# The down pieces of a mixture of experts on a second DMA queue, with rows that lie side by side

## What is computed

```python
def expert_block(args):
    e, tok, wt = args
    xb = h_pad[tok]
    gu = xb @ w_gu[e] + b_gu[e]                      # w_gu: 32 x 1024 x 2048
    gate = jnp.minimum(gu[:, :D_FF], SWIGLU_LIMIT)
    up = jnp.clip(gu[:, D_FF:], -SWIGLU_LIMIT, SWIGLU_LIMIT)
    act = (up + 1.0) * gate * jax.nn.sigmoid(SWIGLU_ALPHA * gate)
    y = act @ w_down[e] + b_down[e]                  # w_down: 32 x 1024 x 1024
    return y * wt[:, None].astype(y.dtype)
```

## Time and profile before

| | |
|---|---|
| median of 3 runs | 1272.31 us (1272.03 to 1273.51) |
| the profiled execution | 1272.04 us, its span 1270.2 us |
| PE busy | 1167.3 us, 92% of the span |
| DVE, ACT, POOL busy | 431.1, 126.8, 93.5 us |
| bytes moved by DMA | 459.96 MB, 362 GB/s over the span |
| queue q1 (SP's) | 458.50 MB |
| queue q10 (ACT's) | 1.08 MB |
| granted clock of PE | 0.984 of full speed on average |

### The profile page before, as it was taken

One profiled execution on the slowest core, in us unless ns is written; L12 is line 12 of the kernel. 1 busy time (PEld: TensorE's weight loads), 2 busy tenths in 40 slices (PEclk: granted clock), 3 DMA queues, 4 the chain that ended last, 5 costly groups with the idle time before them and its releaser, 6 DMA issues.

```text
span 1270.2 us, 17813 instructions
## 1 busy us (share of the span) xinstructions
PE 1167.3 (92%) x6940; PEld 491.0 (39%) x6940; DVE 431.1 (34%) x824; ACT 126.8 (10%) x254; POOL 93.5 (7%) x116
## 2 busy tenths in 40 slices
PE   5999898995999999999999999999999999999997
PEld 1765676853333333333333333333333333333332
DVE  3785784125222233222222222222233222222224
ACT  3101112213100000000000000000000000000001
POOL 1503653002000000000000000000000000000000
PEclk8999899996999999999999999999999999999999
DMA  9999314563899999999999999999999999999991
GB/s 356 367 411 387 108 67 151 190 228 145 324 416 417 418 418 418 418 418 418 418 418 418 417 418 418 418 417 417 417 417 417 417 417 419 418 418 418 414 417 58
DMA packets 95588, 459.96 MB, mean 362 GB/s; under 512 B 13565, under 2 KB 13801, under 8 KB 59721
## 3 DMA queue, kind: packets, MB, share of 16 engines
q1 hardware_dynamic: 93992, 458.50, 89.4%
q10 hardware_dynamic: 1568, 1.08, 0.3%
HBM read 458.51 MB, written 1.05 MB: 362 GB/s over the span
## 4 chain that ended last, share of the span: by engine, by line
PE 45%; DMA 22%; SPq 18%; DVE 2%; issue 2%; ACT 1%; DVEq 0%
DMA ring<-in_w_down 22%; PE ps L762 17%; SPq L334 13%; PE ps L803 8%; SPq L329 5%; PE ps L464 4%; PE ps L745 3%; PE ps L619 2%; PE ps L657 2%; PE ps L687 2%; PE ps L754 1%; PE ps L591 1%; PE ps L784 1%; PE ps L494 1%; PE ps L791 0%
## 5 line engine op out<-in xcount | busy, mean ns | idle before, releaser
L803 PE MATMUL ps<-ring,tmp 128*64 128x512 f32 x1024 | 241.3, 601 | 48.5 <-DMA ring<-in_w_down 38.6
L762 PE MATMUL ps<-ring,zone 128*64 128x512 f32 x1024 | 232.2, 595 | 0.0
L762 PE MATMUL ps<-zone 128*64 128x512 f32 x896 | 207.5, 596 | 0.3 <-DVE zone L1294 0.3
L1340 DVE TENSOR_TENSOR x_tok<-x_tok,ps 128x512 f32<-128x512 f32 x128 | 82.0, 682 | 261.9 <-PE ps L745 261.9
L803 PEld LDWEIGHTS ps<-ring,tmp 128*64 128x64 f32 x1024 | 67.6, 136 | 201.7 <-issue 126.8
L762 PEld LDWEIGHTS ps<-ring,zone 128*64 128x64 f32 x1024 | 70.7, 137 | 151.5 <-issue 151.4
L762 PEld LDWEIGHTS ps<-zone 128*64 128x64 f32 x896 | 61.5, 137 | 136.1 <-issue 134.8
L464 PE MATMUL ps<-hT,ring 128*128 128x256 f32 x448 | 103.1, 390 | 2.7 <-ACT hT L856 2.7
L1334 DVE TENSOR_TENSOR tmp<-ps,zone 128x512 f32<-128x512 f32 x32 | 22.1, 692 | 226.7 <-PE ps L803 226.7
L935 ACT ACTIVATE hT<-hT 128x512 f32<-128x512 f32 x32 | 20.2, 630 | 785.4 <-DVE hT L1353 785.4
L464 PEld LDWEIGHTS ps<-hT,ring 128*128 128x128 f32 x448 | 86.2, 195 | 20.2 <-issue 8.4
(11 more groups left out here) (270 smaller groups left out, 830.1 us busy)
## 6 DMA issues: line engine op xcount, KB each, us to landing
ring<-in_w_gu SPq DMA_DIRECT2D x128, 1024.0 KB, 21.6
ring<-in_w_down SPq DMA_DIRECT2D x128, 1024.0 KB, 24.2
zone<-in_w_gu SPq DMA_DIRECT2D x112, 1024.0 KB, 19.6
ring<-in_w_ada SPq DMA_DIRECT2D x24, 1024.0 KB, 16.5
ring<-in_w_in SPq DMA_DIRECT2D x16, 1024.0 KB, 14.8
xs<-in_w_gu SPq DMA_DIRECT2D x16, 1024.0 KB, 20.4
ring<-in_w_glu SPq DMA_DIRECT2D x4, 1024.0 KB, 11.5
ring<-in_w_out SPq DMA_DIRECT2D x4, 1024.0 KB, 4.8
```

What stands on the lines that cost most here:

```text
L762: last = mm(ps[CAP * h:CAP * h + CAP, b, :], hg[:, j, :], w[:, 0, D * b + 512 * h:D * b + 512 * h + 512], start=False, stop=(j == GU_PIECE ...
L803: last = mm(ps[CAP * h:CAP * h + CAP, 3, :], actT[:, k % 4, k // 4, :], wk[:, 512 * h:512 * h + 512], start=False, stop=(j == DN_PIECES - ...
L1340: V.tensor_tensor(x_tok[:, t, 512 * h:512 * h + 512], x_tok[:, t, 512 * h:512 * h + 512], ps[:, 6 + h, :], ALU.add).then_inc(S["comb_add"], 1)
```

## The change

The down pieces are issued by ACT, which has a DMA queue of its own. ACT does it at the head of each item, ahead of the sigmoid, with the same wait for `w_used`. SP issues only gate/up pieces from item 2 on, in the order of items; the down pieces of item 0 stay with SP. The rows of w_down are spread otherwise: with a row number written as 512h + 4p + q, partition p gets for each piece the two rows q and q + 1 that lie side by side, 8 KB in one run. For the products to fit, transpose j takes every fourth column of `act_`, starting with j. The bytes, the slots and PE's instructions are the same in number and order.

```diff
+    def down_rows(e, j):
+        k = DN_ROWS[j]
+        return w_down[0, bass.ds(e, 1)].rearrange("e (h p q) n -> p (e h) q n", h=2, p=P)[:, k // 4, k % 4:k % 4 + 2, :]
...
             def load_dn(e, j):
-                k = DN_ROWS[j]
-                src = w_down[0, bass.ds(e, 1)].rearrange("e (k p) n -> p (e k) n", p=P)[:, k:k + 2, :]
-                sp.dma_start(dn_slot(j), src).then_inc(dn_in[j], 16)
+                sp.dma_start(dn_slot(j), down_rows(e, j)).then_inc(dn_in[j], 16)
...
-            def next_dn(i, e):
-                for j in range(DN_PIECES):
-                    sp.wait_ge(w_used, i * PASS + (PRE - PASS + GU_PIECES + j + 1))
-                    load_dn(e, j)
-
-            with sp.Fori(1, EXPERTS // 2 - 1) as q:
+            with sp.Fori(1, EXPERTS // 2) as q:
                 next_gu(2 * q, 2 * q, 0)
-                next_dn(2 * q - 1, 2 * q - 1)
                 next_gu(2 * q + 1, 2 * q + 1, 1)
-                next_dn(2 * q, 2 * q)
-            e = EXPERTS - 2
-            next_gu(e, e, 0)
-            next_dn(e - 1, e - 1)
-            next_dn(e, e)
-            next_gu(e + 1, e + 1, 1)
-            next_dn(e + 1, e + 1)
...
-                    last = nc.tensor.transpose(ps[:, j // 2, P * (j % 2):P * (j % 2) + P], act_[:, P * j:P * j + P], ident)
+                    last = nc.tensor.transpose(ps[:, j // 2, P * (j % 2):P * (j % 2) + P], act_[:, :].rearrange("p (n q) -> p q n", q=4)[:, j, :], ident)
...
+            def load_dn(i, e):
+                for j in range(DN_PIECES):
+                    act.wait_ge(w_used, i * PASS + (PRE - PASS + GU_PIECES + j + 1))
+                    act.dma_start(dn_slot(j), down_rows(e, j)).then_inc(dn_in[j], 16)
...
             with act.Fori(1, EXPERTS) as i:
+                load_dn(i, i)
                 item(i)
```

More of the change, by code:

```diff
@@ L385, in _ @@
                             next_gu(2 * q + par, e, par)
-                            next_dn(2 * q + par, e)
             for i in range(TT):
@@ L952, in _ @@
                     with act.If(i < count):
+                        load_dn(i, act.value_load(itab[0:1, bass.ds(i, 1)], min_val=0, max_val=EXPERTS - 1))
                         item(i)
```

## The result

The changed kernel takes 1260.06 us, median of four runs (1258.76 to 1261.54), against 1272.49 us for the kernel before in the same session. The ratio is 0.9902, with a 95% interval of 0.9884 to 0.9919. The prediction was 1260. Its profiled execution took 1260.16 us, with a span of 1258.3 us, 11.9 less than before.

A forecast was written before the change was run, and what follows sets the result against it. The prediction took the DMA stream's bytes and rate to bound the kernel from 350 to 1240 us. 1272.04 less 8.6 for rate and 3.5 for the tail gave 1259.9, said as 1260 us, range 1249 to 1269.

The forecast's parts named there:

- The bound: From 350 to 1240 us bytes and rate set the time; only rate, holes and PE's work after the last byte count.
- The rate term: 8 KB runs for w_down save 0.072 us a piece over 120 pieces from 350 us on: 8.6 us.
- The second queue: PE's four waits for w_down go; each pass's last gate/up piece comes 2.1 us late; the middle moves no time.
- The tail: From the last byte to the end of the down products: 15.0 us instead of 18.5, saving 3.5 us.
- The sum: Whole kernel: 1272.04 - 8.6 - 3.5 = 1259.9, stated as 1260 us; chance 0.58 for 1255 to 1265.
- The transposes: L791's weight loads 16 bytes apart cost 0 to 1.7 us a pass, covered by PE's 2.1 us wait; taken as 0.
- a sign of being wrong: The forecast is wrong if a pass in which PE has no waits lasts longer than 27.7 us.
- Rows alone: Rival: only the faster rate from w_down's new rows holds, the split does nothing; 1263.4 us, chance 0.11.
- tail alone: Rival: only the shorter tail holds, w_down being slow for another reason than its runs; 1268.5 us, chance 0.06.
- The rule on issuing engines: Trainium skill: starting DMAs from several engines saves only sequencer time; by it the split gives nothing, leaving 1263.4 us.

The follow-up runs named there:

- columns side by side: The changed kernel with the transposes of before, taking 128 columns side by side, so its output is another one: 1260.27 us, ratio 0.991.

## Why the prediction was right, step by step

- **The bound.** Right. Rate, holes and tail account for every kernel of the table: 890 us are bytes, and PE's waits in the middle move from one line to another without moving the end.
- **The rate term.** Right in cause, shown twice: new rows alone give 422 GB/s on one queue, and 4 KB runs on the other matrix give 409. Forecast 8.6 us, measured 9.5 with the queue and 8.8 without. Some of the surplus may be the few down pieces before 350 us, which I didn't count.
- **The second queue.** Right on what it moves: PE's waits for w_down gone, the last gate/up piece late, ACT's issues short (four in 5.49 us, at PE's pace). The wait is not one of 2.1 us in each pass but one of 1.2 to 2.5 us in 15 passes of the last 18, and none in the three that follow a fall of the clock. The last of four down pieces comes later than the 21 us after the first slot is free that I took: the four issued from 703.78 to 709.27 us land 9.0, 12.2, 15.5 and 18.7 us after their issues, the last some 24 us after the first issue, still ahead of the next down products at 730.92.
- **The tail.** Right in direction, mis-sized: 2.4 us instead of 3.5. The last gate/up piece began 1.0 us after the last byte where I took 1.6, but from there PE needed 1247.07 - 1231.90 = 15.2 us instead of 13.4. The eight matmuls took 3.39 us instead of 1.89, at a granted clock of 0.50, and the start of the last gate/up piece to the start of the down products took 8.06 us instead of 6.30: the 1.8 us are all there, nearly all of it the clock (0.50 is its lower level, 1.2 GHz). In the profiled execution with columns side by side the clock didn't fall at this place, and its tail is 14.4 us; its other runs took 2 us or more longer, at a lower mean clock (0.973 to 0.976 against 0.980), which suggests that this part of the tail comes and goes between executions. The prediction had no term for the clock.
- **The sum.** The rate brought 0.9 us more than forecast and the tail 1.1 us less. That 1260 was hit to a tenth is luck; the two terms and their order of size are not.
- **The transposes.** Right that they are hidden under PE's waits. Where there is no wait they cost 0.07 us a pass, and by this a pass without waits lasts 27.76 us, over the 27.7 that the prediction named as a sign of being wrong. Nothing else of the argument fails by it: PE is still 2 us faster than the stream. A load takes 211 ns instead of the 140 of the earlier trace rows, as this row of the changed kernel shows (line L779, weight loads):

```profile
L779 PEld LDWEIGHTS ps<-cst,hT x128: 195/211/220, 339.8 to 1239.3; 128*128 128x128 f32 x128
```

  The Trainium skill's note ("SBUF — State Buffer", section "Door 1: The DMA port swizzle") that an access to a new line of 16 bytes pays agrees with this trace: 71 ns for a load of 128 by 128.
- **The rivals.** "Rows alone" and "tail alone" both measured: 1264.7 where I had 1263.4, and 1265.6 where I had 1268.5. Apart the terms are 7.7 + 6.8 = 14.5 us, together 12.2 to 12.4, a difference that lies within the intervals (about 2 us on each of the three). The traces give a reason for which it may be real: with 4 KB packets the down pieces have the smaller share of the engines and come last, which makes the tail shorter than with 8 KB packets (10.7 against 16.1 us in the profiled executions), and the new rows take that back. I had the turns by packet in mind, but priced the tail only for the combined case.
- **The rule on issuing engines.** The Trainium skill ("DMA: Bandwidth & Descriptors", section "Issuing engines are not separate DMA queues") agrees with the traces on the rate: 422 GB/s with one queue and with two. That the split would therefore give nothing did not come out: the queue alone brought 6.8 us. The stream was full before and after (418 and 417 GB/s) and the bytes end only 0.6 us earlier, so these come from the order of landing at the end, as the tail of 10.7 instead of 18.5 us shows.

## What to carry to other kernels

When a stream of loads is full from start to end, engine waits in the middle are no prize: count the bytes, the rate by length of run, the holes at the start, and what is left to do after the last byte. Late in such a stream ask for things in the order in which they are used, so that the consumer holds nothing that it can only work off at its own pace; early, ask for whatever has a free slot, or the stream gets a hole that is paid at the end. A second queue is one way to change the order of landing, and the order of issue on one queue did it better here, 1250.6 against 1260.1 us.

## What the runs showed of the hardware

- Packets of 4 KB and 8 KB: 410 and 422 GB/s on a full stream. Rows 16 KB apart of which each second 8 KB is skipped cost nothing against rows that follow each other.
- With both queues full the engines took turns by packet: 466 to 461 packets with 8 KB on both, 518 of 4 KB to 523 of 8 KB with the queue alone. Pieces of 1 MiB land in 12.7 us on ACT's queue when both carry 8 KB packets, and in 17.3 us when ACT's are 4 KB. The total rate is the same as with one queue (422 and 422 GB/s with the new rows, 417 and 418 with the old).
- PE's granted clock fell to 0.50, its lower level of 1.2 GHz, in some passes behind a single long wait. In the changed kernel from 740 to 1235 us this was so behind four of the ten waits of 1.8 to 2.5 us (those that end at 814.47, 873.82, 993.37 and 1231.90), and the other six passed without it; eight matmuls took up to 3.62 us there instead of 1.94. What decides between them is not shown. Behind waits of 0.5 to 0.7 us in a row, as in the earlier trace rows, the clock stayed at 1.00 from 620 to 1210 us.
- A weight load of 128 x 128 float32 with a stride of 16 bytes takes 211 ns, 140 ns without.
